# A Trainium2 decoder layer: 64-token experts gathered and transposed in pairs

## The reference

```
t = rms_norm(x, norm_ffn_gain)                       # 512 x 1024
group_p = softmax(t @ w_router_group + b)            # top-1 group of 4
sel = (t @ w_router_expert + b)[chosen group]        # 8 experts, top-2
combine[token, expert] = gp * ev / sum(ev)
for e in range(32):
    hid = silu(t @ w_gate[e]) * (t @ w_up[e])        # 1024 -> 256
    out += combine[:, e:e+1] * (hid @ w_down[e])     # 256 -> 1024
out = rms_norm(x + out, final_norm_gain)
```

## Time and profile before

| what | value |
|---|---|
| median of three runs | 794.27 us |
| the profiled execution, its own time | 794.36 us |
| its span | 792.6 us |
| last product of the last expert ends | 764.4 us into the span |
| what follows it (last copy and scatter, load of the expert results, final norm, store) | 28.2 us |
| PE busy over the span | 726.7 us (92%) |
| read from and written to HBM over the span | 173.35 MB |

### The profile page before, as it was taken

The page is one execution under the profiler, slowest core; times in us unless marked ns, Lnnn a source line. Parts: engine busy times, 40 slices in busy tenths (PEclk is TensorE's granted clock), DMA queues, the critical chain, the costliest instruction groups (busy, mean ns, idle before and its releaser), DMA issues.

```text
span 792.6 us, 11110 instructions
## 1 busy us (share of the span) xinstructions
PE 726.7 (92%) x4296; PEld 528.3 (67%) x4296; DVE 330.5 (42%) x591; ACT 292.4 (37%) x536; POOL 211.7 (27%) x193
## 2 busy tenths in 40 slices
PE   3999999998999999999899968999999999979950
PEld 3788888887877888888678857445555454544620
DVE  4259897978773432563693245100000000000007
ACT  6412664661535555534541320212222222212213
POOL 2046342422331412353560002011312122211110
PEclk9999999999999999999999995999999999989985
DMA  8923313030210300209400558999999999999726
GB/s 242 346 71 123 112 71 107 28 119 27 92 42 14 108 2 1 107 21 403 140 3 1 212 229 325 385 401 363 377 398 372 394 387 397 403 385 413 282 99 251
DMA packets 45218, 163.61 MB, mean 206 GB/s; under 512 B 9771, under 2 KB 13883, under 8 KB 32622
## 3 DMA queue, kind: packets, MB, share of 16 engines
q1 hardware_dynamic: 39470, 154.47, 51.8%
q0 software_dynamic: 5696, 8.43, 3.3%
HBM read 151.33 MB, written 22.02 MB: 219 GB/s over the span
## 4 chain that ended last, share of the span: by engine, by line
PE 85%; DVE 5%; ACT 4%; issue 3%; POOL 1%; DMA 1%; POOLq 0%; ACTq 0%; DVEq 0%; SPq 0%
PE bank L421 13%; PE bank L423 12%; PE bank L422 12%; PE bank L893 11%; PE bank L889 7%; PE bank L925 6%; PE bank L878 4%; PE bank L918 4%; PE bank L549 2%; PE bank L903 1%; DVE arena L2239 1%; PE bank L580 1%; PE bank L570 1%; PE bank L752 1%; PE bank L737 1%
## 5 line engine op out<-in xcount | busy, mean ns | idle before, releaser
L1157 POOL TENSOR_TENSOR w_lo<-arena,w_hi 128x1024 fp32r<-128x1024 f32 x36 | 86.1, 2396 | 209.1 <-ACT w_hi L1321 209.1
L421 PE MATMUL bank<-h_hi,w_hi 128*128 128x512 f32 x320 | 128.2, 401 | 0.5 <-DVE arena L1858 0.5
L423 PE MATMUL bank<-h_hi,w_lo 128*128 128x512 f32 x320 | 125.0, 391 | 0.0
L422 PE MATMUL bank<-h_lo,w_hi 128*128 128x512 f32 x320 | 124.6, 389 | 0.0
L893 PE MATMUL bank<-arena 128*64 128x256 f32 x768 | 91.2, 391 | 5.2 <-issue 5.2
L2195 DVE TENSOR_TENSOR arena<-arena,bank 64x256 f32<-64x256 f32 x24 | 9.9, 413 | 174.4 <-ACT arena L1669 174.4
L1770 DVE SCALAR_TENSOR_TENSOR bank<-arena,bank 128x512 f32<-128x512 f32 x116 | 78.7, 750 | 0.1
L893 PEld LDWEIGHTS bank<-arena 128*64 128x64 f32 x768 | 56.2, 140 | 31.3 <-issue 7.7
L423 PEld LDWEIGHTS bank<-h_hi,w_lo 128*128 128x128 f32 x320 | 60.0, 188 | 13.1
L421 PEld LDWEIGHTS bank<-h_hi,w_hi 128*128 128x128 f32 x320 | 60.1, 188 | 12.8 <-DVE arena L1858 0.6
L422 PEld LDWEIGHTS bank<-h_lo,w_hi 128*128 128x128 f32 x320 | 60.2, 188 | 11.7
(11 more groups left out here) (346 smaller groups left out, 1160.3 us busy)
## 6 DMA issues: line engine op xcount, KB each, us to landing
arena<-in_w_expert_gate_dram SPq DMA_DIRECT2D x32, 1024.0 KB
arena<-in_w_expert_up_dram SPq DMA_DIRECT2D x32, 1024.0 KB
arena<-in_w_expert_down_dram SPq DMA_DIRECT2D x32, 1024.0 KB
arena<-in_w_in_dram SPq DMA_DIRECT2D x8, 2048.0 KB, 8.1
arena<-in_x_dram SPq DMA_DIRECT2D x8, 512.0 KB, 7.2
arena<-in_w_in_dram SPq DMA_DIRECT2D x4, 1024.0 KB, 10.6
y_rows<-arena SPq DMA_DIRECT2D x8, 512.0 KB, 10.3
arena<-in_w_out_dram SPq DMA_DIRECT2D x2, 2048.0 KB, 10.7
```

The costliest lines, as they stand in the source:

```text
L421: pe.matmul(o, wh, xh, start=first, stop=False)
L422: pe.matmul(o, wh, xl, start=False, stop=False)
L423: return pe.matmul(o, wl, xh, start=False, stop=last)
L1157: gp.tensor_tensor(as_raw(w_lo[pslot(s)], s), raw(s), as_raw(w_hi[pslot(s)], s).bitcast(F32), ALU.subtract)\
```

## The change

- Two narrow slots that follow each other form a group. One gather brings their 2 x 64 rows into 128 partitions, eight transposes handle both, and one buffer of 128 columns holds the result (`heT_p`). The products still go by slot, each with its 64 of the 128 columns. A wide slot is a group by itself. For this the wide slots become 0, 1, 2, 3, 8, 13, 18 and 23, so that an even number of narrow slots stands between them. Narrow slots fall from 24 gathers to 12.
- "rows" is now one product for all 32 experts. "rows_e" comes from it by two transposes, in place of sixteen products.
- The permutation is made ahead of the rows. `order_i` has a product and a write of its own ("order"), ahead of the sorted rows. The constants `rfix` on POOL are gone; `perm` sorts by plain rank, and a table `col_of` maps a slot to its column.
- The store of `h2T` is gone; the overflow part, if it ran, would read `h2_rows` and transpose again. SP issues gate and up of expert 3 in its place, before its wait for the gather of slot 0.

```diff
-    WIDE = (0, 1, 2, 3, 8, 14, 20, 26)
+    WIDE = (0, 1, 2, 3, 8, 13, 18, 23)
...
+        R_HE = (o2, R_MASK + D)
+        heT = [at(o, KT, CAP) for o in R_HE]
+        heT_p = [at(o, KT, 2 * NARROW) for o in R_HE]
...
-            b = begin("rows", ("idx_ready", 1), 4)
-            wait(pe, "M_onehot", 2)
+            b = begin("rows", ("perm_ready", 3), 4)
             for i in range(2 * NT):
-                ins = pe.matmul(b[0:CAP, 0:2 * NFIX], row_of[:, i // NT, i % NT, :],
-                                codes[:, i // NT, i % NT, :, 0:NFIX], start=(i == 0), stop=(i == 2 * NT - 1))
+                if i % NT == 0:
+                    wait(pe, "M_onehot", 2 + i // NT)
+                ins = pe.matmul(b[0:CAP, 0:2 * NE], row_of[:, i // NT, i % NT, :],
+                                codes[:, i // NT, i % NT, :, :].rearrange("p q e -> p (q e)"), start=(i == 0),
+                                stop=(i == 2 * NT - 1))
             end(ins, "rows", "route_mm")
-            b = begin("rows_e", ("perm_ready", 4), 6)
+            b = begin("order", ("sorted", 2), 5)
+            wait(pe, "perm_ready", 2)
+            pe.matmul(b[0:1, 0:NE], e_col[0:NE, :], perm[0:NE, :], start=True, stop=True)
+            ins = pe.matmul(b[:, NE:2 * NE], ones[0:NE, :], on_diag[0:NE, :], start=True, stop=True)
+            end(ins, "order", "route_mm")
+            b = begin("rows_e", ("perm_ready", 5), 6)
+            wait(pe, "perm_ready", 3)
             for q in range(2):
-                for i in range(2 * NT):
-                    ins = pe.matmul(b[0:NE, q * CAP:(q + 1) * CAP], codes[:, i // NT, i % NT, q, :],
-                                    row_of[:, i // NT, i % NT, :], start=(i == 0), stop=(i == 2 * NT - 1))
+                ins = pe.transpose(b[0:NE, q * CAP:(q + 1) * CAP], rows_r[0:CAP, q, :], ident[0:CAP, 0:CAP])
...
-                if s < NE - 1:
-                    ex_tr(s + 1)
+                if s == groups[group_of[s]][0] and group_of[s] + 1 < len(groups):
+                    ex_tr(group_of[s] + 1)
...
-            wait(sp, "h2T_ready", 2 * NT)
-            sp.dma_start(h2T_keep, h2T.rearrange("p k n -> p (k n)")).then_inc(S["st_h2T"], 16)
+            expert_gu(3, 3)
             wait(sp, "ld_h0", 16)
-            expert_gu(3, 3)
             expert_dn(3, 3)
             wait(sp, "st_h2", 16 * NT)
-            wait(sp, "st_h2T", 16)
             wait(sp, "sorted", 1)
             for s in range(NFIX, NE):
-                e = sp.value_load(order_i[0:1, s:s + 1], min_val=0, max_val=NE - 1)
+                e = sp.value_load(order_i[0:1, col_of[s]:col_of[s] + 1], min_val=0, max_val=NE - 1)
...
-            def heT_copy(s):
-                wait(act, "ex_tr", s + 1)
-                wait(act, "ex_gu", s - 1)
-                if s in WIDE:
-                    for half in range(2):
-                        ins = act.activation(heT[s % 2][:, half * KH:(half + 1) * KH, :],
-                                             bank[half][:, 0:KH * CAP].rearrange("p (k n) -> p k n", k=KH), ACT.Copy)
-                else:
-                    ins = act.activation(heT_n[s % 2], bank[s % 2][:].rearrange("p (k n) -> p k n", k=KT), ACT.Copy)
+            def heT_copy(g):
+                wait(act, "ex_tr", g + 1)
+                if g >= 2:
+                    wait(act, "ex_gu", groups[g - 2][-1] + 1)
+                n = sum(rows_of(s) for s in groups[g])
+                dst = heT if n == CAP else heT_p
+                for half in range(2):
+                    ins = act.activation(dst[g % 2][:, half * KH:(half + 1) * KH, :],
+                                         bank[half][:, 0:KH * n].rearrange("p (k n) -> p k n", k=KH), ACT.Copy)
```

More of the change, by code:

```diff
@@ L273, in hybrid_layer @@
         R_SORT = R_Y + 2 * NT * CAP + 4 * NRT
[L275 to L280, removed]
+        tie_row, key_row, above, perm, on_diag, wide_row = (at(R_SORT + i * NE, NE) for i in range(6))
+        tie_col, e_col, half_col, key_col, rank = (at(R_SORT + 6 * NE + i, 1) for i in range(5))
+        rows_r = at(R_SORT + 6 * NE + 5, 2, NE)
+        rows_e = at(R_SORT + 8 * NE + 5, 2, CAP)
+        both_e = at(R_SORT + 8 * NE + 5 + 2 * CAP, 2, 2, NARROW)
+        assert R_SORT + 8 * NE + 5 + 2 * CAP + 4 * NARROW <= R_Y + 2 * D
         ridx = at(R_UP + NT * D, 2, NE)
@@ L307, in rows_of, with idx_col @@
             return CAP if s in WIDE else NARROW
+        groups, col_of = [], {}
+        for s in range(NE):
+            if s in WIDE:
+                col_of[s] = WIDE.index(s)
+                groups.append((s,))
+            elif groups[-1][0] in WIDE or len(groups[-1]) == 2:
+                col_of[s] = NW + sum(len(g) == 2 or g[0] not in WIDE for g in groups)
+                groups.append((s,))
+            else:
+                col_of[s] = col_of[s - 1] + NPAIR
+                groups[-1] += (s,)
+        group_of = {s: g for g, members in enumerate(groups) for s in members}
+        assert sorted(col_of.values()) == list(range(NE))
+        def idx_col(g):
+            return col_of[groups[g][0]]
         def bc(ap, shape):
@@ L854, in _ @@
             end(ins, "rows_e", "route_mm")
-            b = begin("sorted", ("sorted", 4), 7)
-            wait(pe, "perm_ready", 4)
+            b = begin("sorted", ("sorted", 6), 7)
+            wait(pe, "perm_ready", 5)
             for q in range(2):
-                pe.matmul(b[0:CAP, q * NE:(q + 1) * NE], rows_e[0:NE, q, :], perm[0:NE, :], start=True, stop=True)
-            pe.matmul(b[:, 2 * NE:3 * NE], both_e[0:NE, :, :].rearrange("p a b -> p (a b)"), perm[0:NE, :], start=True,
-                      stop=True)
@@ L861, in _ @@
-            pe.matmul(b[0:1, 3 * NE:4 * NE], e_col[0:NE, :], perm[0:NE, :], start=True, stop=True)
-            ins = pe.matmul(b[:, 4 * NE:5 * NE], ones[0:NE, :], on_diag[0:NE, :], start=True, stop=True)
+                pe.matmul(b[:, q * NE:(q + 1) * NE], both_e[0:NE, q, :, :].rearrange("p a b -> p (a b)"), perm[0:NE, :],
+                          start=True, stop=True)
+            for q in range(2):
+                ins = pe.matmul(b[0:CAP, (2 + q) * NE:(3 + q) * NE], rows_e[0:NE, q, :], perm[0:NE, :], start=True,
+                                stop=True)
@@ L1260, in _, with gather @@
             gp.wait_ge(S["zeroed"], 16 * NZ)
[L1262 to L1270, removed]
+            def gather(g):
+                n = sum(rows_of(s) for s in groups[g])
+                if g >= NHS:
+                    wait(gp, "ex_tr", g - NHS + 1)
+                if g == NFIX:
+                    wait(gp, "sorted", 5)
+                indices = row_idx[0:n, 0, idx_col(g):idx_col(g) + 1]
+                gp.indirect_dma_start(out=hs[g % NHS][0:n, :], out_offset=None, in_=h2_rows,
+                                      in_offset=bass.IndirectOffsetOnAxis(ap=indices, axis=0),
+                                      bounds_check=T - 1, oob_is_err=False).then_inc(S[f"ld_h{g % NHS}"], 16)
             y_half = y_rows.rearrange("r (h n) -> (r h) n", h=NH2)
@@ L1704, in _ @@
             with act.If(fv > 0):
+                for k in range(KT):
+                    act.wait_ge(S["h2T_again"], k + 1)
+                    act.activation(h2T[:, k, :], bank[k][:], ACT.Copy).then_inc(S["h2T_ready"], 1)
                 with act.Fori(0, NE) as e:
@@ L2154, in _ @@
[L2154 to L2161 removed]
+            o = src[0:CAP, 2 * NE:4 * NE].rearrange("p (a b) -> p a b", a=2)[:, :, NFIX:NW]
```

129 lines of the change are left out of this document (67 added, 62 removed).

## The result

Four runs of the changed kernel had a median of 784.78 us (782.21 to 785.58), beside 794.11 us for four of the kernel before (793.59 to 796.01). The ratio is 0.986, with a 95% interval of 0.984 to 0.989: 9 to 13 us faster. On a second chip job the changed kernel gave 784.16 (781.6 to 784.87) beside 795.58 for the kernel before.

The account below looks back on a forecast made before the run. The weight stream was taken to bound the kernel, with PE's saving worth nothing. 794.36 us less 4.5 of kept lead plus 0.5 for the clock gave 790.4, by the median 790.3 us; 80% range 786.0 to 794.5.

Parts of the forecast that it names:

- What bounded the kernel: Experts' part: the weight stream needs 8.6 us a slot against PE's 7.75 and sets the end from slot 24 on.
- Pairs on PE: Narrow slots: 11.9 us less PE work, costed at nothing, since it turns into longer waits for weights.
- Rival 3: Narrow slots: PE's saving counts in full, needing a faster stream, perhaps through pairs' gathers; 782 us; chance 5%.
- its sign: End of the experts' part: PE has no more waits than before, or the last product ends before 755 us.
- The store: Weight queue before the first gather: 5.3 us of stream saved, plus 1 us from the earlier gather, about 6.3 us.
- How much survives: Wide slots 0 to 3: of the stream's 6.3 us lead, 4.5 us is kept; bounds 1.0 and 6.3.
- The slack that I had given to the slowest engine: Down weights of slot 8: 5 us on the slowest DMA engine, 1 us on the average one; 4.0 taken.
- Rival 1: Wide slots: lead lost to 1 us slack, or slot 0 no earlier, or low clock; 792 to 794.5 us; 22%.
- Routing: Before slot 0: its gather comes 1.0 us earlier; after clock loss PE ends slot 0 0.5 us earlier.
- The end: From slot 31's weights on: unchanged, 8.3 us to the last product, 28.2 after; low clock adds 0.5 us.
- the slower rival: Slots 28 to 31: the clock stays low, 4.6 us more a slot; four give 808 us, two 799; chance 9%.

## Why the prediction was wrong

*What bounded the kernel.* Right: the stream set the end. (The page's DMA row was misread at one place, without consequence: the slice from 475.6 to 495.4 us stands at 8, not 9.) But I read it as the only limit, and it was the first of two that lie close together. The PE work of 7.75 us a slot that I worked out stood only 0.9 us below the stream's 8.63.

*Pairs on PE.* This is the step that failed, in its sentence "The stream is untouched by it: the same weights, rows and padded row entries". The rows and bytes are the same; the number of partitions that a gather names is not, and with it changes how long the weight packets beside it take. Weights and rows move at 408 to 409 GB/s in place of 389 to 393. Widening the gathers was worth 6.8 us by itself and then ran into PE. The saving of 11.9 us on PE, which I had put at nothing, is worth some 3.5 to 5.5 us there: 3.5 from 787.69 to 784.16, a step that also holds the missing store and the routing, and 5.5 by the run with PE's work back. Then the stream bound again. How many transposes PE saves was right; what they are worth depended on the other step. Rival 3, at 5%, named the right outcome and a stream that gets faster through the pairs' gathers, and its sign came: the last product ended at 751.1 us, before 755. Its reason (that they load the slowest engine less) was not tested.

The falls stood in the trace of before. I had read the rate from one stretch of 81 us, 393 GB/s at full share, and took it for the limit. Cut into slices of 1.5 us the same stretch shows 425 and 300, and asks why.

*The store.* SP issued gate and up of expert 3 at 470.45, 2.1 us later than the 468 forecast, as the mixer was, so the 5.3 us of the store are gone from the stream. But the gap at 489 to 493 stayed, since the loads ahead of it are done and the next ones still wait for the gather's landing; of the 1 us that I had added for it the two traces of the changed kernel show 0.6 and nothing (the share of 0.61 and 0.46 over six microseconds, against 0.51).

*How much survives.* I took 4.5 us. In the changed kernel the runs show 0.9, not to be told from nothing, in the kernel before 2.9 (1.4 to 4.5). The slack that I had given to the slowest engine doesn't show: on the average of the engines 1.0 us of lead is left where slot 8's down load is issued. Rival 1 came closest at this step: the kernel before without the store, 792.2 us, is in its range.

*Routing.* The gather of slot 0 comes 1.4 us sooner (I took 1.0). PE's slot 1 starts 0.7 us sooner in the first profile and 0.3 us later in that of the second job (counted from the last store of the tokens), so the 0.5 us is inside what differs from run to run. Slot 0's first product did lose to the clock what I had taken: 9.23 and 9.07 us against 8.75.

*The end.* In the first profile the clock fell once among the last slots, behind the wait of 2.69 us, and the product of slot 28 took 5.36 us for 3.60; the mean granted clock from 718 to 722 us was 0.82. In the second profile it also fell behind a wait of 1.97 us, right at slot 31 (5.36 us for the product), where the first profile kept it up behind 1.96 (3.67 us). So 0.5 us was a fair value for a loss that is nothing in one profile and 1.7 us in the other, and the slower rival did not come. The Trainium skill ("TensorE: Matmul & The Clock Gate", "HAM oscillation — how this bites in real kernels") has a product stream that waits for its operands throttled at every wait, in a kernel with longer waits (about 3 to 5 us). The traces here agree for the waits of 2.60 to 4.11 us, all seven, and for only some of the shorter ones.

*A mechanism for the width?* The runs show that 64, 96 and 112 partitions slow the weight packets and 128 don't, and that scatters, which read SBUF, leave them alone, the wide ones with their 96 partitions included (no fall behind the one at 635.2 us). The Trainium skill ("DMA: Bandwidth & Descriptors", "The descriptor swizzle") states that in a transfer to 128 partitions each engine writes to one port of SBUF. A gather over 64 or 96 partitions that is spread over the same engines would then write to ports that belong, for the weights, to other engines. That fits the runs with 64, 96 and 128, but no run measured a port, so it is argued and not shown. Nor do I know why 112 partitions leave some engines so late.

## What to carry to other kernels

Where small indexed gathers run beside a wide stream of loads, give them the partition count of the loads, 128, with out-of-bounds indices in the rows that aren't needed; here it cost POOL 0.05 us an issue and gave 6.8 us. A rate read over a long stretch at full DMA share is not yet the limit: look at slices as short as one gather's fall. When a second limit stands close behind the first (here 7.75 us a slot behind 8.63), cost no saving at nothing; a lead in a stream, on the other hand, is worth only what the next wait for a free buffer leaves of it.

## What the runs showed of the hardware

- A gather over 64 or 96 partitions slows the 8 KB packets of other loads 4.5 to 6 us behind its issue: they take 410 to 490 ns in the mean in place of 314, for 1 to 1.5 us with 64 partitions and 3 to 4 us with 96, and the core's rate falls from about 425 to about 300 GB/s with a DMA share of 1.02 all the while. A busy share doesn't show this. Over 128 partitions none of this is seen (18 of 6025 packets at 400 ns and more from 560 to 690 us, 676 of 5600 before).
- With 128 partitions an issue costs POOL little more: 1.02 us against 0.97.
- Gathers over 112 partitions were the worst of all, 808.6 us.
- Waits of 1.6 to 2.1 us ahead of a product sometimes cost PE its clock (1.62, 1.96 and 2.06 us: 5.36 us for 32 matmuls) and sometimes not (1.61, 1.96 and 2.02 us: 3.67 us). The seven waits of 2.60 to 4.11 us in these traces all cost it.
